# A tuned transformer kernel: the first layer's modulation computed in five parts, and attention queries made two heads ahead with part of the work on GpSimd

## The chip, the cores and the metric

The kernel runs on one core of a Trainium2 chip. The metric is the device time of one launch in microseconds. Three runs of the kernel before gave 2015.85, 2015.19 and 2012.34 us, so the median is 2015.19 us. A difference of 0.2% is 4.0 us.

## The reference, cut to what matters

Two blocks run one after the other on 256 latent and 256 context tokens of width 1024, in float32. The first block has four layers; layer 0 mixes tokens by a Fourier transform, layer 1 by differential attention, layer 2 by latent attention with 16 heads, layer 3 by a Fourier transform again. The second block has one mixer and a mixture of experts. The change touches two places: the modulation vectors of layer 0, and the attention of layer 2.

```python
sh_a, sc_a, g_a, sh_m, sc_m, g_m = split(silu(c) @ mod_w[i] + mod_b[i], 6)   # c: 1024, mod_w[i]: 1024 x 6144
h = rms_norm(x, g_mix) * (1 + sc_a) + sh_a                # shift and scale ahead of the mixer
y = fft2(h, axes=(token, channel within group of 256)).real @ fourier_w + bias     # layer 0
x = x + g_a * y                                           # gate
x = x + g_m * (relu((rms_norm(x, g_mlp) * (1 + sc_m) + sh_m) @ w1) ** 2 @ w2)
# layer 2, for each of 16 heads (96-wide queries and keys, 64-wide values, 256 queries, 512 keys)
p = softmax((q_nope k_nope^T + q_rope k_rope^T) * scale);  o = p @ v
```

The same is computed for the context with silu(c_ctx). The shift of layer 0 is constant over the tokens, so in the transform it reaches only token 0 of the result.

## The kernel before, in words

All activations lie transposed: 128 channels on the partitions, 8 column tiles, 512 tokens (256 latent, 256 context) along the free axis. A float32 product is made from three products of rounded halves (`split_product`, L1847 to L1849: high times high, high times low, low times high). Weights come in 1 MB units of two 128-column panels; ScalarE rounds a panel to its high half (`split_hi`, L1064, 1.05 us), VectorE subtracts for the low half (`split_lo`, L2818, 1.22 us), and TensorE multiplies 24 times per panel. Every engine's program is written out in order, with semaphores; nothing is rescheduled. All loads go through the one queue of SyncE, in the order of its program, each held until its buffer is free.

**Layer 0 before.** The start turns the inputs and normalises the token rows. Then TensorE alternates between `first_rows_product` (L2032; 16 products that fold the tokens) and `mod_unit` (L1890 to L1901): one unit is 1 MB of `mod_w`, 128 input channels by 2048 output columns, as four products of 512 columns in four column groups, put into one PSUM bank. Eight units give shift and scale of the mixer together (group 0). `copy_first_rows` (ScalarE, L1190), `turn_first` (TensorE, L1908) and `first_read` (VectorE, L2982 to L2993) bring them to the partitions. Only then can ScalarE and VectorE scale the folded rows (`G_hi`, L1237, `G_lo`, L3051), with the shift put into two edge columns of each half (`edge`). The transform over channels follows: 8 steps of 12 matmuls, each followed by one unit of group 1 (gate of the mixer and scale of the MLP), while ScalarE copies and rounds (L1250, L1254), VectorE combines cosines and sines (L3071 to L3074) and GpSimd makes the low halves `H_lo` (L1027). Next come the 8 panels of `fourier_w`: panels 0 to 3 whole, panels 4 to 7 once for the latent and once for the context half (`half_outputs`). During them `boundary` on VectorE adds the gated result to x (L2886), sums squares (L2838), splits the next panels and runs `mod_folds` (L2971): a multiply-accumulate of one 128x1024 tile of the transposed `mod_w` with the spread `c`, which makes 128 modulation values for one stream. 32 of these make shift and gate of the MLP in layer 0; 4 stand ahead of `boundary`, 12 in it, 16 in the MLP. The MLP of layer 0 starts with `half_products` on three panels; its first output tile is read at 149.41 us.

SyncE's order before: c and mod_b (3 small loads), x, ctx, units 0 to 2, the other vectors, units 3 and 4, the store of c, dft, units 5 to 15, then the four loads of `fourier_w`, the spread c, 4 units for the folds, and the MLP weights.

**Latent attention before.** A turn for head h does on VectorE: `m_max` of two score tiles (L3493), `query(h+1)` (L3461), a wait for the two exponentials, 1/z (L3502), the scaling of the first half of the probabilities (L3504), `query_lo(h+1)` (L3465), low halves of keys (L3471), of the output of head h-2 (L3514), of the turned probabilities of head h-1 (L3522), in eight places of values (L3477) and after turns 0, 1, 3, 6, 8, 14, 15 a `split_lo` of a panel. ScalarE does the exponentials (L1569), the high halves, and the scaling of the second half of the probabilities (L1577). TensorE makes scores(h) (which wait for `query_lo(h)`), query(h+1), keys, the weighted values of h-2, and turns the probabilities of h-1 (L2396). GpSimd is idle.

Of the kernel before, what the change touches and what calls it, by code (L numbers as in the profile page):

```python
# [6 lines left out]
F32 = mybir.dt.float32  # L7
F32R = mybir.dt.float32r
# [45 lines left out]
def place_vectors():  # L54
    rows = [0] * VEC_TILES
    plan = [("mod_b_lo", 0, 96), ("c", 0, 8), ("c_ctx", 0, 8), ("mod_b_hi", 1, 96),
            ("norm_mix_g", 2, 32), ("norm_mlp_g", 2, 32), ("final_g", 2, 8), ("fourier_b", 2, 16),
# [113 lines left out]
def mla_tiles():  # L171
# [10 lines left out]
    for turn in range(MLA_HEADS - 1):  # L182
        add("q", turn + 1, "mla_q", turn + 2)
# [137 lines left out]

def mla_bank(n):
# [60 lines left out]
FIRST_GROUPS = 2  # L383
FIRST_TILES = MOD_TILES // 3
FIRST_COLS = FIRST_TILES * P
FIRST_PART = FIRST_COLS // 4
FIRST_UNITS = FIRST_GROUPS * KT
FIRST_RING = 3
ROWS_AFTER = {1: range(0, 3), 2: range(3, 6), 3: range(6, 9), 4: range(9, 12), 5: range(12, 14), 6: range(14, 16)}
# [6 lines left out]
LATER_FIRST = {"shift_m": 3 * KT, "gate_m": 5 * KT}  # L396


def place_mods():


    tiles = [(0, t) for part in ("shift_m", "gate_m") for t in range(LATER_FIRST[part], LATER_FIRST[part] + KT)]
# [14 lines left out]
    take("first", [(0, 4)])  # L417
    take("four0", enumerate([2, 2, 2, 2, 1, 1, 1, 1]))
# [25 lines left out]
def build_program(nc, a, out):  # L444
# [8 lines left out]
    with ctx:  # L453
# [51 lines left out]
        first_raw = [sb(f"first_raw{r}", [P, FIRST_COLS], over=work + r * 4 * FIRST_COLS) for r in range(FIRST_RING)]  # L505
        assert FIRST_RING * FIRST_COLS <= MOD_RING * MOD_PAIR * D
        c_all = sb("c_all", [P, 2, D])
        mod_prod = sb("mod_prod", [P, D])
        c_rows = sb("c_rows", [2 * KT, P], over=at["mod_prod"] + 4 * FIRST_PART)
# [12 lines left out]
        edge = norm_buf[3][:, 0:4 * KT].rearrange("p (t e) -> p t e", e=2)  # L522
# [3 lines left out]
        first_rows = sb("first_rows", [P, FIRST_PART], over=at["mod_prod"])  # L526
# [33 lines left out]
        mq_f = sb("mq_f", [P, LAT])  # L560
        mq_hi, mq_lo = sb("mq_hi", [P, LAT], F32R), sb("mq_lo", [P, LAT], F32R)
# [108 lines left out]
        mod_ps = psum[4]  # L670
# [23 lines left out]
        def inner(v, m, st):  # L694

            return v[:, m, st * LAT:(st + 1) * LAT].rearrange("p (e c) -> p e c", e=2)[:, :, 1:]

        def edges(v):

            return v[:, :, :].rearrange("p m (s e c) -> p (m s) e c", s=2, e=2)[:, :, :, 0]  # L700
# [21 lines left out]
        first_w = a["mod_w"][0].rearrange("(k p) (t c) -> k p t c", p=P, t=3 * 2)  # L722
        first_t = [slice(0, 2), slice(2, 5, 2)]
# [26 lines left out]
        def _(sp):  # L750
# [21 lines left out]
            def load_mod(n):  # L772

                if n < MOD_RING:
                    sp.wait_ge(s("first_used"), FIRST_UNITS)
# [11 lines left out]
            def load_mlp(layer, region_free=None):  # L787
# [18 lines left out]
                if layer == 0:  # L806
                    block(0, "w0 w1 w2 m1 w3 m1 w4 w5 m1 w6 m1 w7 m1")
# [25 lines left out]
            rows = {"mod_b_lo": mod_b[0:96], "mod_b_hi": mod_b[96:192],  # L833
# [12 lines left out]
            def load_first(units):  # L846
                for n in units:
                    if n >= FIRST_RING:
                        sp.wait_ge(s("first_used"), n - FIRST_RING + 1)
                    sp.dma_start(first_raw[n % FIRST_RING][:, :].rearrange("p (t c) -> p t c", t=2),  # L850
                                 first_w[n % KT][:, first_t[n // KT], :]).then_inc(s(f"first_in{n % FIRST_RING}"), 16)
# [9 lines left out]
            load_first(range(FIRST_RING, KT - 3))  # L861
            sp.wait_ge(s("c_rows"), 2)
            sp.dma_start(c_store.rearrange("(r c) -> r c", c=P), c_rows[:, :]).then_inc(s("c_all"), 16)
# [3 lines left out]
            load_first(range(KT - 3, KT))  # L867
            four_w = a["fourier_w"][0].rearrange("(k p) (u c) -> u p k c", p=P, c=2 * P)
            load_first(range(KT, FIRST_UNITS))
            for u in range(2):  # L870
                load_unit(PLAN.at["four0"]["unit"] + u, [(whole, four_w[u])])
# [3113 lines left out]
```

## Time and profile before

| | us |
|---|---|
| median of three runs | 2015.19 |
| the profiled execution's own time | 2013.53 |
| its span in the profile | 2011.8 |
| TensorE busy | 1921.9 (96% of the span) |
| VectorE busy | 1531.0 (76%) |
| ScalarE busy | 1018.4 (51%) |
| GpSimd busy | 22.5 (1%) |
| mean granted TensorE clock | 0.984 of full |
| DMA | 346.67 MB, mean 172 GB/s |

The busy shares are over the whole span; a change in one stage has to be read from that stage, so the rows below come from 0 to 150 us (layer 0) and from 1148 to 1258 us (latent attention). Line numbers are those of the kernel before. "PEclk" is the share of full TensorE clock that was granted.

### The profile page before, as it was taken

Reading aid. Unit: us, or ns where it says so; the run is one execution under the profiler, and the core shown is the slowest. Engines: PE = TensorE matmul, PEld = TensorE weight load, DVE = VectorE, ACT = ScalarE, POOL = GpSimd, SP = SyncE. Lnnn points to the kernel's source line nnn. Section 1 sums busy time; section 2 is a strip of 40 time slices with the busy share of each in tenths; the row PEclk is TensorE's granted clock in tenths of the full one; section 3 lists DMA queues with packets and bytes.
Section 4 is the critical chain, followed back from the end, with each engine's and each line's share of the span. In section 5 each row is a group of like instructions: output and inputs, shape, how many; then the busy total and the mean of one; then the engine's idle time right before and its main releaser. Section 6 shows DMA issues by size and latency. Waiting matters only on the chain.

```text
span 2011.8 us, 31051 instructions
## 1 busy us (share of the span) xinstructions
PE 1921.9 (96%) x11602; PEld 1684.5 (84%) x11602; DVE 1531.0 (76%) x2619; ACT 1018.4 (51%) x1721; POOL 22.5 (1%) x40
## 2 busy tenths in 40 slices
PE   6889999999999999999999777999999999999998
PEld 4687888889787888888888667999999999997886
DVE  3689888887667758777777588788887667876796
ACT  5353323245666656232333577655555546655685
POOL 0200000000000000000000100000000000000000
PEclk9999999999999999999999899999999999999999
DMA  7936455541211234557675220677645555426795
GB/s 291 321 119 232 165 209 188 188 168 48 84 64 63 67 112 139 169 186 244 236 244 158 58 73 27 227 268 261 207 135 189 168 169 168 134 67 236 260 354 195
DMA packets 265319, 346.67 MB, mean 172 GB/s; under 512 B 24167, under 2 KB 234962, under 8 KB 263778
## 3 DMA queue, kind: packets, MB, share of 16 engines
q1 hardware_dynamic: 265186, 344.90, 51.2%
q8 instruction: 84, 1.38, 0.3%
q14 instruction: 49, 0.40, 0.1%
HBM read 343.81 MB, written 1.06 MB: 171 GB/s over the span
## 4 chain that ended last, share of the span: by engine, by line
PE 75%; DVE 10%; ACT 6%; issue 5%; SPq 1%; DMA 1%; DVEq 0%; ACTq 0%
PE bank L1847 23%; PE bank L1848 23%; PE bank L1849 23%; PE bank L2663 2%; DVE w_lo L2818 2%; PE bank L2653 1%; ACT p_raw L1401 1%; ACT p_raw L1389 1%; DVE p_all L3297 1%; ACT norm L1157 1%; ACT w_hi L1064 1%; ACT mp_raw L1569 1%; DVE x L2886 1%; DVE neg_max L3306 1%; DVE norm L2844 1%
## 5 line engine op out<-in xcount | busy, mean ns | idle before, releaser
L2818 DVE TENSOR_TENSOR w_lo<-w_raw,w_hi 128x1024 fp32r<-128x1024 f32 x449 | 545.6, 1221 | 51.6 <-ACT w_hi L1064 24.9
L1064 ACT ACTIVATE w_hi<-w_raw 128x1024 fp32r<-128x1024 f32 x350 | 368.0, 1053 | 381.7 <-PE bank L1849 371.2
L1847 PE MATMUL bank<-h_hi,w_hi 128*128 128x512 f32 (+3 forms) x1360 | 466.9, 343 | 14.7 <-DVE w_lo L2818 8.6
L1848 PE MATMUL bank<-h_lo,w_hi 128*128 128x512 f32 (+3 forms) x1360 | 460.3, 338 | 0.0
L1849 PE MATMUL bank<-h_hi,w_lo 128*128 128x512 f32 (+3 forms) x1360 | 459.9, 338 | 0.0
L1847 PE MATMUL bank<-g_hi,w_hi 128*128 128x256 f32 (+1 forms) x1216 | 401.6, 330 | 7.2 <-DVE g_lo L3351 3.6
L1848 PE MATMUL bank<-g_lo,w_hi 128*128 128x256 f32 (+1 forms) x1216 | 399.6, 329 | 0.0
L1849 PE MATMUL bank<-g_hi,w_lo 128*128 128x256 f32 (+1 forms) x1216 | 399.5, 329 | 0.0
L1847 PEld LDWEIGHTS bank<-h_hi,w_hi 128*128 128x128 f32 x1360 | 257.9, 190 | 50.5 <-DVE w_lo L2818 10.8
L1849 PEld LDWEIGHTS bank<-h_hi,w_lo 128*128 128x128 f32 x1360 | 258.1, 190 | 27.7
L1848 PEld LDWEIGHTS bank<-h_lo,w_hi 128*128 128x128 f32 x1360 | 258.2, 190 | 26.4 <-issue 0.3
L1847 PEld LDWEIGHTS bank<-g_hi,w_hi 128*128 128x128 f32 x1216 | 231.8, 191 | 30.2 <-DVE g_lo L3351 4.5
L1849 PEld LDWEIGHTS bank<-g_hi,w_lo 128*128 128x128 f32 x1216 | 231.8, 191 | 20.3
L1848 PEld LDWEIGHTS bank<-g_lo,w_hi 128*128 128x128 f32 x1216 | 231.9, 191 | 19.7
L2971 DVE CUSTOM_DVE_ANT_0 mod_raw<-mod_raw,c_all,vec 128x1024 f32<-128x1024 f32 x160 | 203.0, 1278 | 0.0
L3016 DVE SCALAR_TENSOR_TENSOR x<-bank,mod,x 128x256 f32<-128x256 f32 x192 | 87.4, 479 | 85.1 <-PE bank L1849 79.8
L1304 ACT ACTIVATE norm<-bank 128x512 f32<-128x512 f32 x64 | 38.3, 598 | 189.4 <-PE bank L1849 189.4
L1744 ACT ACTIVATE w_hi<-w_raw 128x1024 fp32r<-128x1024 f32 x99 | 104.1, 1059 | 33.8 <-PE bank L1849 22.5
L3164 DVE TENSOR_TENSOR norm<-norm 128x512 f32<-128x512 f32 (+1 forms) x128 | 71.0, 555 | 54.2 <-ACT norm L1304 49.6
L2971 DVE CUSTOM_DVE_ANT_0 mod_prod<-mod_raw,c_all,vec 128x1024 f32<-128x1024 f32 x80 | 102.2, 1277 | 0.0
L3167 DVE TENSOR_TENSOR g_lo<-norm,g_hi 128x512 fp32r<-128x512 f32 (+1 forms) x128 | 71.5, 559 | 13.6 <-DVE norm L3164 0.5
L1847 PE MATMUL bank<-u_hi,w_hi 128*128 128x258 f32 x256 | 73.5, 287 | 0.0
(535 smaller groups left out, 2832.0 us busy)
## 6 DMA issues: line engine op xcount, KB each, us to landing
w_raw<-in_mlp_w SPq DMA_DIRECT2D x128, 1024.0 KB, 5.4
mod_raw<-in_mod_t SPq DMA_DIRECT2D x80, 1024.0 KB, 7.3
w_raw<-in_w_expert_gate SPq DMA_DIRECT2D x34, 512.0 KB, 4.7
w_raw<-in_w_expert_up SPq DMA_DIRECT2D x34, 512.0 KB, 5.8
w_raw<-in_w_expert_down SPq DMA_DIRECT2D x17, 1024.0 KB, 5.7
first_raw<-in_mod_w SPq DMA_DIRECT2D x16, 1024.0 KB, 5.9
w_raw<-in_diff_w_qkv SPq DMA_DIRECT2D x12, 1024.0 KB, 5.2
w_raw<-in_fourier_w SPq DMA_DIRECT2D x8, 1024.0 KB, 7.9
```

Of the source, the lines that this page charges most:

```text
L1064: act.activation(split_panel(W_hi[n % RING], n), raw_panel(n), ACT.Copy).then_inc(s("w_hi"), 1)
L1304: act.activation(relu[j % 2][:, 0:n_cols], bank[(t0 + j) % BANKS][:, 0:n_cols], ACT.Relu).then_inc(s("relu"), 1)
L1744: act.activation(W_hi[(p0 + n) % RING][:, :], raw_panel(p0 + n), ACT.Copy).then_inc(s("w_hi"), 1)
L1847: pe.matmul(dst, w_hi, r_hi, start=start, stop=False)
L1848: pe.matmul(dst, w_hi, r_lo, start=False, stop=False)
L1849: return pe.matmul(dst, w_lo, r_hi, start=False, stop=stop)
L2663: ins = pe.matmul(slot_out[half][:, :], e[x % 2][:, k, 0:P], v[:, w], start=x % 4 == 0 and k == 0 and q == 0, stop=x % 4 == 3 and k == 1 a ...
L2818: dve.tensor_tensor(split_panel(W_lo[n % RING], n), raw_panel(n), split_panel(W_hi[n % RING], n).bitcast(F32), ALU.subtract).then_inc(s("p ...
L2971: dve.tensor_tensor_reduce(mod_prod[:, :] if again else raw, raw, c_all[:, st, :], 1.0, bias, ALU.mult, ALU.add, mod[layer][:, t, st:st + ...
L3016: ins = dve.scalar_tensor_tensor(X[:, m, c], bank[t % BANKS][:, c], mod[layer][:, gate_at + m, st:st + 1], X[:, m, c], ALU.mult, ALU.add)
L3164: dve.tensor_tensor(squared, relu[j % 2][:, c], relu[j % 2][:, c], ALU.mult).then_inc(s("g_sq"), 1)
L3167: dve.tensor_tensor(G_lo[:, j, c], squared, G_hi[:, j, c].bitcast(F32), ALU.subtract).then_inc(s("g_lo"), 1)
```

## The change

**Layer 0.** The modulation is cut into five parts of 1024 columns in the order scale and shift of the mixer, gate of the mixer, shift and scale of the MLP (`FIRST_PARTS = [KT, 0, 2*KT, 3*KT, 4*KT]`). A unit is still 1 MB but holds 256 input channels by 1024 columns, so a part has 4 units and all have 20 (16 before), and a unit is 8 products of 256 columns in place of 4 of 512. The shift of the MLP is no longer folded on VectorE: 16 folds (4 ahead of `boundary`, 12 in it) are gone; the gate of the MLP stays folded, in the MLP. Units 0 to 6 stand among the row products, unit 7 after step 1 of the transform, units 8 to 19 among the panels. The parts alternate over three banks (psum 4 to 6). The shift goes in by itself: it is multiplied by the DFT matrix (`shift_wave`) and added to the first token's column, which is kept in `first_col` and split apart from the rest; TensorE waits for it (`edge` >= 3) before the first panel. The `edge` steps are gone. ScalarE's split of dft comes after all 16 row copies (after 14 before); four panels are split ahead of `boundary` (three before). The first vector tile takes the two norm vectors too, so 5 small loads stand ahead of x (3 before). SyncE issues the first two `fourier_w` units after unit 7, the other two after unit 10, units 11 to 19 after them, and then the spread c and three fold units behind the first MLP weights.

**Latent attention.** Queries are made two heads ahead with two buffers each. The scaling of the second half of the probabilities goes from ScalarE to GpSimd, and the seven low halves of panels from VectorE to GpSimd.

```diff
-plan = [("mod_b_lo", 0, 96), ("c", 0, 8), ("c_ctx", 0, 8), ...
+plan = [("mod_b_first", 0, 48), ("c", 0, 8), ("c_ctx", 0, 8), ("norm_mix_g", 0, 32), ("norm_mlp_g", 0, 32), ...
+FIRST_PARTS = [KT, 0, 2 * KT, 3 * KT, 4 * KT]
+FIRST_AFTER = {0: [8, 9], 1: [10, 11], 2: [12, 13], 3: [14, 15, 16], 4: [17], 5: [18], 6: [19]}
-ROWS_AFTER = {1: range(0, 3), 2: range(3, 6), 3: range(6, 9), 4: range(9, 12), 5: range(12, 14), 6: range(14, 16)}
+ROWS_AFTER = {1: range(0, 4), 2: range(4, 8), 3: range(8, 12), 4: range(12, 14), 5: range(14, 16)}
-    take("first", [(0, 4)])
-    take("four0", enumerate([2, 2, 2, 2, 1, 1, 1, 1]))
 # SyncE
-            load_first(range(KT - 3, KT))
-            load_first(range(KT, FIRST_UNITS))
+            load_first(range(5, 8))
             for u in range(2):
                 load_unit(PLAN.at["four0"]["unit"] + u, [(whole, four_w[u])])
+            load_first(range(8, 11))
             sp.wait_ge(s("u_lo"), 4 + GROUPS)
             for u in range(2, 4):
                 load_unit(PLAN.at["four0"]["unit"] + u, [(whole, four_w[u])])
+            load_first(range(11, FIRST_EACH * len(FIRST_PARTS)))
+            sp.wait_ge(s("edge"), 3)
 # TensorE
+            def first_unit(n):
+                part, u = n // FIRST_EACH, n % FIRST_EACH
...
+                for i in range(FIRST_STEP):
+                    for j in range(4):
+                        ins = pe.matmul(first_ps[part % 3][32 * j:32 * (j + 1), 0:FIRST_SIDE], silu_c[:, k, :], ...
-                    mod_unit(n, 1)
+                    if n == 1:
+                        first_unit(2 * FIRST_EACH - 1)
+                    if n == 2:
+                        turn_first(1)
+                    if n == 3:
+                        shift_wave()
+                pe.wait_ge(s("edge"), 3)
                 for m in range(4):
                     panel_product(n0 + m, t + m, H_hi, H_lo, ...)
-                    if m == 0:
-                        turn_first(1)
+                    for u in FIRST_AFTER[m]:
+                        first_unit(u)
+                    if m == 1:
+                        turn_first(2)
 # VectorE, end of the transform
-                for n in range(1, AHEAD):
+                dve.wait_ge(s("wave"), 1)
+                dve.wait_ge(s("four_sum"), KT)
+                for half in range(2):
+                    dve.scalar_tensor_tensor(col, wave, DFT_N ** 0.5, col, ALU.mult, ALU.add).then_inc(s("edge"), 1)
+                split_lo_at(p0 + 1)
+                dve.wait_ge(s("first_col"), 1)
+                dve.tensor_tensor(first_tokens(H_lo), first_col, first_tokens(H_hi), ALU.subtract).then_inc(s("edge"), 1)
+                for n in range(2, RING):
                     split_lo_at(p0 + n)
 # GpSimd, latent attention
+            for turn in range(MLA_HEADS):
+                pool.wait_ge(s("z_inv"), BEFORE_MLA["z_inv"] + turn + 1)
+                pool.tensor_scalar(mp_raw[turn % 2][1][:, :], mp_raw[turn % 2][1][:, :], m_zinv[:, turn % 2, 1:2], None,
+                                   ALU.mult).then_inc(s("mla_norm1"), 1)
+                for n in MLA_SPLITS.get(turn, []):
+                    pool.wait_ge(s("w_hi"), p0 + n + 1)
+                    pool.tensor_tensor(split_panel(W_lo[r], p0 + n), raw_panel(p0 + n), ..., ALU.subtract)
 # VectorE, ScalarE, TensorE, latent attention
-                    if turn + 1 < MLA_HEADS:
-                        query(turn + 1)
+                    if turn + 2 < MLA_HEADS:
+                        query(turn + 2)
```

## Rows read from the trace of the kernel before

**Rows 1.** The page: busy us, share of the span and instructions of each engine.
```profile
PE 1921.9 (96%) x11602; PEld 1684.5 (84%) x11602; DVE 1531.0 (76%) x2619; ACT 1018.4 (51%) x1721; POOL 22.5 (1%) x40
```
**Rows 2.** Stretch, its us, busy us of PE, PEld, DVE, ACT, POOL, PEclk, DMA share, GB/s.
```profile
45.00:51.00 6.00, 5.95 (x25) 4.09 (x26) 2.54 (x9) 1.54 (x5) 0.00 (x0) 0.50 0.06 10
...
69.50:73.65 4.15, 0.00 (x1) 0.01 (x1) 1.28 (x2) 1.61 (x3) 0.00 (x0) 0.74 1.09 349
...
90.00:122.00 32.00, 25.32 (x155) 22.64 (x155) 30.70 (x54) 8.81 (x13) 0.00 (x0) 0.95 0.67 230
```
**Rows 3.** Waits from 0 to 220 us: who waited for whom, total, times, longest.
```profile
PE bank L1847 <- DVE w_lo L2818: 8.6, 5, 4.2
...
ACT w_hi L1064 <- DMA w_raw<-in_fourier_w: 6.3, 1, 6.3
```
**Rows 4.** SyncE's queue in order of time: start, us, the transfer issued.
```profile
5.82 0.47 SPq L843 DMA_DIRECT2D vec_rows<-in_norm_mix_g  x1
6.33 0.42 SPq L843 DMA_DIRECT2D vec_rows<-in_norm_mlp_g  x1
...
61.41 9.64 SPq L761 DMA_DIRECT2D w_raw<-in_fourier_w  x4
```
**Rows 5.** Folds in 90 to 122 us, one row of two forms.
```profile
L2971 DVE CUSTOM_DVE_ANT_0 mod_raw<-mod_raw,c_all,vec 128x1024 f32<-128x1024 f32 x7 | 8.9, 1277 | 0.0
```
**Rows 6.** The chain of waits in order of time, one of eight modulation units in the transform.
```profile
57.30 1.00 PE bank L1899 x8
```
**Rows 7.** ScalarE's and VectorE's instructions in order of time, end of the row products.
```profile
36.42 1.05 ACT L1221 ACTIVATE dft_hi<-dft 128x1024 fp32r<-128x1024 f32 x1
...
37.50 1.23 DVE L3272 TENSOR_TENSOR dft_lo<-dft,dft_hi 128x1024 fp32r<-128x1024 f32 x1 [12.67 <-ACT dft_hi L1221]
...
42.66 1.70 ACT L1237 ACTIVATE g_hi<-four_raw,scale_mix 128x254 fp32r<-128x254 f32 x4 [1.66 <-issue]
```
**Rows 8.** The same view, VectorE's last four scaled low halves in the transform.
```profile
59.97 2.70 DVE L3051 SCALAR_TENSOR_TENSOR g_lo<-four_raw,scale_mix,g_hi 128x254 fp32r<-128x254 f32 x4 [1.10 <-ACT g_hi L1237]
```
**Rows 9.** Instructions in order of time: GpSimd and VectorE at one time.
```profile
52.33 1.28 POOL L1027 TENSOR_TENSOR h_lo<-norm,h_hi 128x512 fp32r<-128x512 f32 x1 [50.33 <-ACT h_hi L1254]
...
52.72 0.91 DVE L3073 TENSOR_TENSOR norm<-norm 128x2 f32<-128x2 f32 x1
53.55 0.15 DVE L3074 TENSOR_TENSOR norm<-norm 128x2 f32<-128x2 f32 x1
```
**Rows 10.** VectorE in latent attention, in order of time: first, three middle, last turn.
```profile
1152.14 0.69 DVE L3493 TENSOR_REDUCE m_max<-bank 128x1 f32<-128x512 f32 x1 [1.07 <-PE bank L1849]
...
1220.30 1.28 DVE L3493 TENSOR_REDUCE m_max<-bank 128x1 f32<-128x512 f32 x2
...
1225.85 1.28 DVE L3493 TENSOR_REDUCE m_max<-bank 128x1 f32<-128x512 f32 x2
...
1228.25 0.49 DVE L3504 TENSOR_SCALAR mp_raw<-mp_raw,m_zinv 128x512 f32<-128x512 f32 x1
1228.65 0.42 DVE L3465 TENSOR_TENSOR mq_lo<-mq_f,mq_hi 128x256 fp32r<-128x256 f32 x1
...
1231.95 1.28 DVE L3493 TENSOR_REDUCE m_max<-bank 128x1 f32<-128x512 f32 x2
...
1250.07 1.28 DVE L3493 TENSOR_REDUCE m_max<-bank 128x1 f32<-128x512 f32 x2
```
**Rows 11.** Groups by line in latent attention: busy, mean ns, idle before and releaser.
```profile
L1847 PE MATMUL bank<-mk_hi,mq_hi 128*128 128x512 f32 x31 | 14.3, 461 | 13.7 <-DVE mq_lo L3465 13.7
...
L1577 ACT ACTIVATE mp_raw<-mp_raw,m_zinv 128x512 f32<-128x512 f32 x16 | 11.5, 720 | 0.4 <-DVE m_zinv L3502 0.2
...
L2818 DVE TENSOR_TENSOR w_lo<-w_raw,w_hi 128x1024 fp32r<-128x1024 f32 x7 | 8.6, 1225 | 0.6
...
L3477 DVE TENSOR_TENSOR h_lo<-bank,h_hi 128x512 fp32r<-128x512 f32 x8 | 5.3, 681 | 0.3 <-ACT h_hi L1551 0.3
```
**Rows 12.** ScalarE in order of time: the first output tile of the MLP of layer 0.
```profile
149.41 0.60 ACT L1304 ACTIVATE norm<-bank 128x512 f32<-128x512 f32 x1 [1.18 <-PE bank L1849]
```

More of the change, by code:

```diff
@@ L181, in mla_tiles @@
     add("k", 0, "mla_k_lo", 2)
-    for turn in range(MLA_HEADS - 1):
-        add("q", turn + 1, "mla_q", turn + 2)
+    add("q", 1, "mla_q", 2)
+    for turn in range(MLA_HEADS - 2):
+        add("q", turn + 2, "mla_q", turn + 3)
         if turn % 2 == 0 and turn // 2 + 1 < MLA_HEADS // 2:
@@ L395 @@
 MOD_STEPS = {}
-LATER_FIRST = {"shift_m": 3 * KT, "gate_m": 5 * KT}
 def place_mods():
-    tiles = [(0, t) for part in ("shift_m", "gate_m") for t in range(LATER_FIRST[part], LATER_FIRST[part] + KT)]
+    tiles = [(0, t) for t in range(5 * KT, MOD_TILES)]
     tiles += [(layer, t) for layer in range(1, DEPTH) for t in range(MOD_TILES)]
@@ L521, in build_program @@
         row_sum, row_inv = o_sum[:, 0:4], o_inv[:, 0:4]
-        edge = norm_buf[3][:, 0:4 * KT].rearrange("p (t e) -> p t e", e=2)
+        first_rows = [sb(f"first_rows{r}", [P, FIRST_SIDE], over=at["mod_prod"] + 2048 + r * 4 * FIRST_SIDE) for r in range(2)]
+        first_col = sb("first_col", [P, KT, 2])
         lam_in = sb("lam_in", [1, 4, HALF])
@@ L1169, in boundary @@
                         square(name, TOK, m - 1, x0 + m)
+                    if m == 0 and name == "mlp0":
+                        copy_first_rows(2)
                 split_hi(n0 + 4 + AHEAD)
@@ L1595, in mla_attention @@
                         values(i)
-                    for n in splits.get(turn, []):
+                    for n in MLA_SPLITS.get(turn, []):
                         if n == 4:
@@ L1888, in first_products @@
                         norm_sum(*norm)
-            def mod_unit(u, g):
-                if u == 0 and g:
-                    pe.wait_ge(s("mod_read"), g)
-                n = KT * g + u
-                pe.wait_ge(s(f"first_in{n % FIRST_RING}"), 16 * (n // FIRST_RING + 1))
-                for j in range(4):
-                    ins = pe.matmul(mod_ps[32 * j:32 * (j + 1), 0:FIRST_PART], silu_c[:, u, :],
-                                    first_raw[n % FIRST_RING][:, j * FIRST_PART:(j + 1) * FIRST_PART],
-                                    start=(u == 0), stop=(u == KT - 1))
-                ins.then_inc(s("first_used"), 1)
@@ new lines, in turn_first, with shift_wave @@
+            def turn_first(part):
+                pe.wait_ge(s("first_rows"), part + 1)
+                for j in range(FIRST_SIDE // P):
+                    ins = pe.transpose(first_ps[part % 3][:, j * P:(j + 1) * P], first_rows[part % 2][:, j * P:(j + 1) * P],
+                                       ident[:, :])
+                ins.then_inc(s("first_turned"), 1)
+            def shift_wave():
+                pe.wait_ge(s("mod_sum"), 2)
+                for half in range(2):
+                    for k in range(2):
+                        ins = pe.matmul(wave_ps[:, half * KT:(half + 1) * KT], dft[:, 2 * k, half * P:(half + 1) * P],
+                                        mod[0][:, k:KT:2, :], start=(k == 0), stop=(k == 1))
+                ins.then_inc(s("wave"), 1)
@@ L1961, in half_outputs @@
                         ins.then_inc(s("half_done" if st == 0 else "tile_done"), 1)
+                        if name == "mlp0" and st == 0:
+                            for u in FIRST_AFTER.get(m, []):
+                                first_unit(u)
+                            if m == 5:
+                                turn_first(3)
+                            if m == KT - 1:
+                                turn_first(4)
             def half_products(n0, t0, name):
@@ L2895, in boundary @@
                         add_square(name, TOK, m - 1)
-                    mod_folds(*folds(m))
+                    if name == "mix1":
+                        mod_folds(("mlp", 0, BLOCKS - 1), KT + m)
                 split_lo_at(n0 + 4 + AHEAD)
@@ L2903, in boundary @@
                     add_square(name, LAT, m - 1, 0)
-                    mod_folds(*folds(m))
                 add_square(name, LAT, KT - 1, 0)
+                if name == "mlp0":
+                    first_read(3)
+                    first_read(4)
                 if name == "mix1":
@@ L3524, in mla_attention @@
                         values(i)
-                    for n in splits.get(turn, []):
-                        split_lo_at(p0 + n)
             norm_rest("mix2", TOK)
```

255 lines of the change are left out of this document (129 added, 126 removed).

## The prediction

> **What bounds the kernel now.** I read the page first. TensorE is busy for 96% of the span, so a change can win only where TensorE idles or runs at its lower clock, and whatever it adds to TensorE in a full stretch costs its whole length [rows 1]. Then the busy time by stretch in layer 0 [rows 2]. Three holes stand there. From 69.5 to 73.65 us TensorE does nothing. From 90 to 122 us it is busy for 25.3 of 32 us, an idle 6.7, while VectorE is busy for 30.7: that stretch is bound by VectorE. And the granted clock is 0.50 from 45 to 51 us (the 1.2 GHz level of 2.4, after four almost idle microseconds), and 0.95 on average in 90 to 122, which is 32 x 0.05 = 1.6 us of lost work. The waits name the causes: TensorE waits for low halves of panels, 4.2 us at once, and behind it ScalarE waits 6.3 us for `fourier_w` [rows 3]. SyncE issues that load only at 61.41, behind all sixteen modulation units [rows 4]. In 90 to 122 us the folds take 7 x 1.28 us in one of their two forms, 14 in all [rows 5]: 18 of VectorE's 31 us.
>
> In latent attention VectorE leads: turns without a panel split take 5.55 us (from 1220.30 to 1225.85) or 6.10 us (to 1231.95), the 15 turns from 1152.14 to 1250.07 take 97.9 us, and TensorE waits 13.7 us for the low half of the query [rows 10, 11].
>
> **Ahead of the transform.** Two more small loads, 0.5 us apart, stand ahead of x [rows 4]; the first row product waits for ctx behind x, so everything shifts by +0.95. In the stage of row products one unit fewer stands: a unit takes 1.0 us [rows 6], with the change of operands about 1.2, so -1.2. The turn of part 0 comes behind the twelfth product, and TensorE waits there for a row copy and the copy of the sums: +0.9 of waiting and 0.35 of transposes where the old turn was after everything. The last row copy ends some 0.7 us later than before, at 39.85. Now ScalarE's split of dft (1.05) comes after it, then VectorE's (1.15 of 1.23 until the next can start), then the reading of part 0 (0.4): the first scaled row at 42.45 in place of 42.66 [rows 7]. The early scale is thus hidden by nothing: the dft split takes its place as the last wait. With the edge steps gone the transform starts at about 44.75, after 45.05: -0.3 so far. TensorE still idles nearly 4 us ahead of it, so I leave the slow clock of 45 to 51 as it is.
>
> **The transform.** Seven of eight units leave it, 8.4 us of TensorE. But the steps hang on ScalarE (per two steps: four scalings 1.7, copies 0.7, roundings 1.2, 3.6 us) and on VectorE, whose four low halves take 2.70 us beside GpSimd [rows 8], and TensorE only catches up with them. The last scaled rows come at about 61.05, 1.7 us ahead of 62.7. Then, in order: sums of steps 4 and 5 (1.6), first panel high and low (2.2), sums of 6 and 7 (1.6), the wave added (0.4), first tokens rounded (0.25), panel 1 high (1.05) and low (1.2), first tokens' low half (0.2): 8.5 us of instructions and, with semaphores and GpSimd in the way once, 9.4 to 11. The first panel starts between 70.5 and 72.1; I take 71.3 against 73.65. So of the 4.2 us hole, which the earlier `fourier_w` load closes, most comes back as the wait for `edge` >= 3, behind which all panels queue. Up to here: -2.35. The slow clock after the hole stays, since the hole stays.
>
> **The panels.** The 16 folds leave (4 ahead of `boundary`, 12 in it), and with them the idle 6.7 us and the 1.6 us of slow clock [rows 2]: -8.3. But twelve units now stand here, on an engine with no idle time left to hide them: 12 x 1.2 = +14.4. A unit has twice as many matmuls of half the width; the ends are 1.0 us, the row of before, and 2.0 us, if each matmul keeps its time [rows 6]; 1.2 lies nearest the row, since the columns streamed are the same. Three turns replace one, with a wait of 0.5 for the copy of part 2: +1.0. The panels: +7.1, with ends of +4.7 and +16.7. DMA hides: each unit is issued when the third before it is used, 7 us or more ahead of its own use, except 17 to 19, where it is about 6; if that cover goes it is 1 or 2 us. In the MLP behind it nothing moves: its folds and the first weights stand as far ahead of their use as before. Layer 0 in sum: -2.35 + 7.1 = +4.75.
>
> **Latent attention.** The seven splits leave VectorE: 7 x 1.15 = 8.0 us [rows 11]. Queries two heads ahead end the wait of 13.7 us on TensorE; that saves VectorE only what it waits itself, the 0.55 by which every second turn is longer [rows 10]. The new 15 turns, at 5.55, plus eight value splits of 0.6 [rows 11], less 1.45 for the shorter turns 0, 1 and 14, are 86.6 us: -11.3. ScalarE loses 16 scalings of 0.72, 0.62 apart [rows 11]; at the end, where TensorE waits for the last low halves, this gives 0.8: -12.1. Against it stands the new neighbour. In the transform a VectorE addition of two columns with both inputs in SBUF, 0.15 us right behind it, took 0.91 us, from 52.72 to 53.63, while a GpSimd subtraction ran from 52.33 to 53.61 [rows 9]: it waited for GpSimd's end. The new GpSimd scaling becomes free to start at 1/z, as VectorE's own scaling does (1228.25), and right behind that stands the low half of the query (1228.65, both inputs in SBUF) [rows 10]. So VectorE waits for GpSimd's whole scaling, in every turn. Nothing in the trace is that scaling. The ends are 0, if GpSimd is late and slips in behind the query's low half, and 1.28 us, the two-input row of the same shape [rows 9]; I take 0.75, above half of that row, as it reads one input in place of two. 15 x 0.75 = +11.2. The GpSimd splits, 2.6 us each, fall on instructions of VectorE that read PSUM: nothing. Attention: -0.9, with ends of -12.1 and +7.1.
>
> The Trainium skill, SBUF — State Buffer, section Who interferes with whom, says the two share a port pair as an exclusive lock, held for the instruction, against VectorE instructions with two SBUF inputs or in a two-port mode; the 0.91 us agrees, and it speaks against this change. The Trainium skill, GPSIMD Engine Reference, section 3.1, gives a two-input loop 2.6 cycles per element and the shortest one-input bodies 1.03, at 1.2 GHz: 0.44 us for 512 elements, an estimate without dispatch. By it attention would come to -12.1 + 6.6 = -5.5 and the kernel to no gain or loss; no row here shows it.
>
> **The sum.** +4.75 - 0.9 = +3.9 us. The profiled execution took 2013.53 (span 2011.8 and 1.7 around it), so 2017.4; the median of the runs is 1.7 above that execution, so the prediction is 2019.1.
>
> **The rivals.**
> - Slower clearly: GpSimd's scaling takes the full 1.28 and VectorE pays it in 15 turns. For it: rows 9. Against: one input. It decides above 0.81 us (12.1 / 15), where attention turns into a loss. +7.1 + 4.75 = +11.9: 2027.
> - Faster clearly: GpSimd slips in behind the query's low half, so the lock costs nothing. For it: a start only 0.4 us late does it. Against: GpSimd started 0.1 us after its releaser in the transform. -12.1 + 4.75 = -7.4: 2007.8.
> - Layer 0 does better: the transform runs with TensorE ahead and the first panel starts at 68.5, and a unit costs 1.0. For it: the row of 1.0. Against: the list of instructions behind the last scaled rows. -5.1 + 4.7 = -0.4, attention -0.9 to -5.5: 2011 to 2014.
> - The stall only moves: units 14 to 19 arrive late behind `fourier_w` and each other, 1 us each: +6 more, 2025. For it: DMA at 1.09 of its share in the hole [rows 2]; against: three buffers ahead.
>
> **How the numbers follow.** Forecast 0.40 (own range 2015 to 2023), slower rival 0.18, faster rival 0.15, better layer 0 0.17, late units 0.10. What a measurement of this kernel can tell from no change is 0.2%, 4 us: 2011.2 to 2019.2. The forecast lies at that edge and gives half its chance to each side, so slower is 0.20 + 0.18 + 0.10 = 0.48, less 0.06 for what I may have missed in favour: 0.42; faster is 0.15, 0.05 of the third rival and those 0.06: 0.26; the same 0.32. The range of 2007 to 2027 runs from the faster to the slower rival and leaves out less than 2 in 10.
>
> **What would show it.** TensorE's first panel near 71 us, led by the low half of the first tokens; VectorE no longer full in the panels, TensorE without idle time there, and `half_products` some 5 us later (first tile of the MLP read near 154 us, before at 149.4 [rows 12]). In attention turns of 6.3 us, all alike, with the query's low half over 1 us long. The prediction is wrong if the panels start before 69 us, if the first MLP tile is read before 150, or if turns are 5.6 us (faster) or 6.8 (slower).

## The result, and the profile after

The changed kernel takes 2001.07 us (median of 4 runs, 2000.89 to 2001.83), the kernel before 2013.76 (median of 4): a ratio of 0.9932, 95% interval 0.992 to 0.9945. That is 12.7 us less. I had forecast 2019.1, in a range from 2007 to 2027: wrong in sign and outside the range. (My forecast stood on three runs of the kernel before; the fourth lowers their median from 2015.19 to 2013.76.)

The page of the changed kernel, its engine line (busy us, share of the span, instructions):
```profile
PE 1921.4 (96%) x11804; PEld 1689.5 (85%) x11804; DVE 1501.7 (75%) x2573; ACT 1006.8 (50%) x1705; POOL 72.1 (4%) x63
```
TensorE is busy for as long as before [rows 1], in a span of 1999.3 us in place of 2011.8, so what left is idle time. GpSimd went from 22.5 to 72.1 us.

The same stretches as in [rows 2], and latent attention (stretch, its us, busy us of PE, PEld, DVE, ACT, POOL, PEclk, DMA share, GB/s):
```profile
69.50:73.65 4.15, 2.77 (x7) 2.19 (x8) 3.60 (x4) 1.33 (x2) 0.15 (x1) 0.50 0.00 0
90.00:122.00 32.00, 30.56 (x272) 23.75 (x271) 16.53 (x38) 7.37 (x13) 0.00 (x0) 1.00 0.89 325
1152.00:1257.00 105.00, 93.10 (x618) 82.65 (x618) 81.63 (x169) 69.57 (x159) 49.90 (x23) 0.98 0.15 49
```
In the panels VectorE has gone from 30.70 to 16.53 busy us, and TensorE's 6.7 idle us are 1.4. In latent attention TensorE is busy for 93.1 of 105 us (84.5 before).

To see where the time went I set equal instructions of the two traces side by side and took the difference of their starts. Behind layer 0 the changed kernel is 3.3 us late (first MLP tile, below, against [rows 12]). Ahead of latent attention it is 5.3 us late. Behind it, from the MLP of layer 2 on, it is 10.4 us early, so attention gave 15.7 us. At the end it is 12.5 early. So 2.0 us were lost and 2.1 won in places where nothing was changed.

The 2.0 us between layers 0 and 2 lie in two such places. Here are those stretches, of the changed kernel and then of the one before:
```profile
516.00:560.00 44.00, 40.88 (x221) 32.74 (x222) 30.03 (x72) 29.42 (x70) 0.00 (x0) 0.96 0.15 49
630.00:680.00 50.00, 49.25 (x271) 40.83 (x270) 35.44 (x76) 33.16 (x77) 0.00 (x0) 0.93 0.19 64
```
```profile
516.00:560.00 44.00, 39.54 (x230) 31.53 (x226) 30.84 (x74) 28.64 (x69) 0.00 (x0) 1.00 0.16 50
630.00:680.00 50.00, 48.33 (x284) 39.19 (x285) 36.32 (x77) 35.39 (x84) 0.00 (x0) 1.00 0.20 64
```
The granted clock was 1.00 before and 0.96 and 0.93 after, over unchanged instructions that start 3 to 5 us later. It does not go with the change: `layer0` and `dft_spread` (below), which have layer 0's part too, show 1.00 in both stretches, while `attn_scale_act` and `attn_low_later`, whose layer 0 is that of the kernel before, show 0.96 in the first. (The 0.93 of the second stretch stands in two of the five kernels with layer 0's part, and in none of the others.) The 2.1 us won back are mostly the same thing the other way round: from 1640 to 1665 us the kernel before has a granted clock of 0.93, the changed one has 1.00 over the same instructions and gains 1.5 us there. What makes the clock fall in one execution and not in another is not shown. A single trace tells parts apart only down to some 2 us unless one looks at this column.

Layer 0 of the changed kernel in order of time (start, us, engine, line, tiles, idle time before and its releaser): a unit pair in the panels, the late unit, and the first MLP tile:
```profile
70.88 0.80 PE L1866 MATMUL bank<-h_hi,w_hi 128*128 128x512 f32 x1 [7.13 <-DVE h_lo L3120]
...
86.75 1.93 PE L1920 MATMUL bank<-first_raw,silu_c 128*32 128x256 f32 x32
...
109.87 1.07 PE L1920 MATMUL bank<-first_raw,silu_c 128*32 128x256 f32 x16 [1.44 <-DMA first_raw<-in_mod_w]
```
```profile
152.74 0.60 ACT L1328 ACTIVATE norm<-bank 128x512 f32<-128x512 f32 x1 [1.19 <-PE bank L1868]
```

And one turn of latent attention, VectorE and then GpSimd, for [rows 10]. Turns in which VectorE makes no low half of values take 5.27 and 5.51 us (plain turns, below). From VectorE's first row maximum (`m_max`, one pair in each turn) to the sixteenth it is 82.9 us, 97.9 before:
```profile
1222.65 0.17 DVE L3548 RECIPROCAL m_zinv<-m_z 128x2 f32<-128x2 f32 x1 [0.58 <-ACT mp_raw L1592]
1222.85 0.49 DVE L3550 TENSOR_SCALAR mp_raw<-mp_raw,m_zinv 128x512 f32<-128x512 f32 x1
1223.25 0.42 DVE L3509 TENSOR_TENSOR mq_lo<-mq_f,mq_hi 128x256 fp32r<-128x256 f32 x1
1223.70 0.69 DVE L3516 TENSOR_TENSOR mk_lo<-bank,mk_hi 64x512 fp32r<-64x512 f32 x1
...
1225.97 1.28 DVE L3539 TENSOR_REDUCE m_max<-bank 128x1 f32<-128x512 f32 x2
```
```profile
1222.91 2.11 POOL L1048 TENSOR_SCALAR mp_raw<-mp_raw,m_zinv 128x512 f32<-128x512 f32 x1 [3.14 <-DVE m_zinv L3548]
...
1239.21 1.86 POOL L1048 TENSOR_SCALAR mp_raw<-mp_raw,m_zinv 128x512 f32<-128x512 f32 x1 [3.41 <-DVE m_zinv L3548]
```
GpSimd's scaling runs from 1222.91 to 1225.02, longer than I had allowed at its worst (1.28), and VectorE works beside it as if it were not there: the low half of the query takes 0.42 us as before. GpSimd is the slower one for it: 2.11 us where that low half stands beside it, 1.86 and 1.85 in the last two turns, which have none.

### The profile page after: what moved, and what is told of

It is laid out like the page before. It is cut to its first block, busy times and chain, and to the rows that moved or that the text cites. A ratio compares the mean times of both kernels' runs of the same rounds, so it can differ in the third digit from the quotient of the medians.

```text
span 1999.3 us, 31406 instructions
## 1 busy us (share of the span) xinstructions
PE 1921.4 (96%) x11804; PEld 1689.5 (85%) x11804; DVE 1501.7 (75%) x2573; ACT 1006.8 (50%) x1705; POOL 72.1 (4%) x63
## 4 chain that ended last, share of the span: by engine, by line
PE 79%; DVE 10%; ACT 5%; issue 4%; DMA 1%; POOL 1%; SPq 0%; DVEq 0%; ACTq 0%
PE bank L1866 24%; PE bank L1867 23%; PE bank L1868 23%; PE bank L2712 2%; PE bank L2702 1%; DVE w_lo L2867 1%; ACT p_raw L1424 1%; PE bank L1920 1%; ACT p_raw L1412 1%; ACT norm L1173 1%; DVE p_all L3341 1%; ACT mp_raw L1592 1%; DVE mpt_lo L3568 1%; DVE norm L2893 1%; ACT w_hi L1080 1%
## 5 line engine op out<-in xcount | busy, mean ns | idle before, releaser
L2867 DVE TENSOR_TENSOR w_lo<-w_raw,w_hi 128x1024 fp32r<-128x1024 f32 x442 | 538.0, 1223 | 44.0 <-ACT w_hi L1763 21.9
L3019 DVE CUSTOM_DVE_ANT_0 mod_raw<-mod_raw,c_all,vec 128x1024 f32<-128x1024 f32 x152 | 192.9, 1279 | 0.0
L3019 DVE CUSTOM_DVE_ANT_0 mod_prod<-mod_raw,c_all,vec 128x1024 f32<-128x1024 f32 x72 | 92.0, 1278 | 0.0
```

The source lines that it names most:

```text
L2867: dve.tensor_tensor(split_panel(W_lo[n % RING], n), raw_panel(n), split_panel(W_hi[n % RING], n).bitcast(F32), ALU.subtract).then_inc(s("p ...
L3019: dve.tensor_tensor_reduce(mod_prod[:, :] if again else raw, raw, c_all[:, st, :], 1.0, bias, ALU.mult, ALU.add, mod[layer][:, t, st:st + ...
```

## The experiments

Times are medians; ratios are against the kernel before, run beside them, with their 95% interval. The runs were made in four batches, in which the median of the kernel before was 2013.66 to 2014.67 us. So a difference of two medians from different batches is good to about 1 us.

**The two parts apart.** `layer0` and `attn` are the kernel before with one part of the diff each.

> The kernel before with the layer 0 part of the change alone, latent attention as before. If the 3.3 us that stand behind layer 0 in the changed kernel's trace are this part's price: before plus 3.3, 2017. The forecast on record said plus 4.75. A further 2 us appear between 510 and 650 us of that trace, where nothing was changed and the granted clock was 0.98 against 1.00: if they belonged to the change, this kernel would be 5.3 us slower, 2019; I expect them to be absent or as large in the kernel before of another execution.

Measured: 2017.08 us, ratio 1.0019 (1.0009 to 1.0029). Its trace is 3.3 to 3.4 us late from the first MLP on, up to latent attention.

> The kernel before with the latent attention part of the change alone: queries two heads ahead, GpSimd scaling the second half of the weights and splitting the seven panels. Layer 0 is as before. From the trace of the changed kernel (first ScalarE tile of layer 3's attention 5.3 us later than before, the first MLP tile behind it 10.4 us earlier) I expect 15.7 us less than before, 1998. My forecast on record gave this part 0.9 us, its faster rival 12.1 us (2001.7). First and sixteenth maxima of VectorE 83 us apart, low half of a query 0.42 us long.

Measured: 1997.09 us, ratio 0.9916 (0.9903 to 0.9929). The first and sixteenth maxima are 83.2 us apart. The parts add up: layer 0 costs 3 to 4 us, attention gives 16 to 17. All the gain is in attention. `attn` alone is 4.0 us under the changed kernel, though the intervals of the two ratios overlap.

**Does GpSimd hold VectorE?**
`attn_two_inputs` is `attn` with the scaling on GpSimd written in another form, with 1/z as a second tensor:
```
-                pool.tensor_scalar(mp_raw[turn % 2][1][:, :], mp_raw[turn % 2][1][:, :], m_zinv[:, turn % 2, 1:2], None,
-                                   ALU.mult).then_inc(s("mla_norm1"), 1)
+                pool.tensor_tensor(mp_raw[turn % 2][1][:, :], mp_raw[turn % 2][1][:, :],
+                                   m_zinv[:, turn % 2, 1:2].to_broadcast([P, TOK]), ALU.mult).then_inc(s("mla_norm1"), 1)
```


> As attn, but GpSimd scales by a tensor_tensor with 1/z broadcast, so that it reads two inputs from SBUF, and not by a tensor_scalar. Theory (the form of GpSimd's instruction decides: two tensors from SBUF hold VectorE, one does not): the low half of a query, 0.42 us in attn, lasts until GpSimd's end, 0.9 us or more, and a turn is 0.5 us or more longer: 7 to 8 us slower than attn, about 2006. Rival (GpSimd gives way to VectorE whatever its form): low half 0.42 us, turns of 5.3 to 5.5 us as in attn, the same time; it would be up to nothing but GpSimd's own length.

Measured: 2012.08 us, ratio 0.9989 (0.998 to 0.9999), 15 us over `attn`. VectorE and GpSimd in one turn:
```profile
1202.74 0.17 DVE L3517 RECIPROCAL m_zinv<-m_z 128x2 f32<-128x2 f32 x1 [0.59 <-ACT mp_raw L1585]
1202.94 1.37 DVE L3519 TENSOR_SCALAR mp_raw<-mp_raw,m_zinv 128x512 f32<-128x512 f32 x1
1204.23 0.41 DVE L3478 TENSOR_TENSOR mq_lo<-mq_f,mq_hi 128x256 fp32r<-128x256 f32 x1
```
```profile
1202.99 1.04 POOL L1048 TENSOR_TENSOR mp_raw<-mp_raw,m_zinv 128x512 f32<-128x512 f32 x1 [1.12 <-DVE m_zinv L3517]
```
GpSimd starts 0.05 us behind VectorE, as in `attn` (0.06), yet now VectorE's own scaling takes 1.37 us in place of 0.49 and ends 0.28 us behind GpSimd. That is so in fifteen of the sixteen turns, and fifteen times 0.88 is 13.2; the turns are 96.4 us together in place of 83.2. In the first turn GpSimd starts 0.12 us behind VectorE's scaling, and there it is the other way round: VectorE keeps its 0.49 us, and GpSimd takes 1.27. I had named the wrong victim, the query's low half, and so the size was too small (7 to 8), but the theory stands: the form of GpSimd's instruction decides. GpSimd's two-input form is also the faster one for GpSimd, 1.04 against 1.86 to 2.11 us.

`attn_two_after` is `attn_two_inputs` with GpSimd's start moved:
```
-                pool.wait_ge(s("z_inv"), BEFORE_MLA["z_inv"] + turn + 1)
+                pool.wait_ge(s("mla_norm0"), turn + 1)
+                pool.wait_ge(s("qk_lo"), BEFORE_MLA["qk_lo"] + min(turn + 3, MLA_HEADS))
```


> As attn_two_inputs, but GpSimd starts its scaling only behind VectorE's scaling and the query's low half, the two instructions of VectorE in the turn whose tensors all lie in SBUF; what VectorE does meanwhile reads a bank. Theory (GpSimd's two-input instruction holds only VectorE's instructions that work from SBUF alone): VectorE's scaling is 0.49 us again, its other instructions keep their lengths, GpSimd's scaling takes 1.04 us and ends no later than the 2.1 us one of attn: turns of 5.3 to 5.5 us and the time of attn, 1997 (1996 to 1998). Rival (the hold is against anything VectorE does): mk_lo or the halves behind it are up to 1 us longer, turns of 6.1 us or more, about 2012.

Measured: 1997.62 us, ratio 0.9918 (0.9905 to 0.993), turns of 5.26 and 5.51:
```profile
1211.88 0.48 DVE L3520 TENSOR_SCALAR mp_raw<-mp_raw,m_zinv 128x512 f32<-128x512 f32 x1
1212.28 0.42 DVE L3479 TENSOR_TENSOR mq_lo<-mq_f,mq_hi 128x256 fp32r<-128x256 f32 x1
1212.61 0.68 DVE L3486 TENSOR_TENSOR mk_lo<-bank,mk_hi 64x512 fp32r<-64x512 f32 x1
1213.21 0.41 DVE L3530 TENSOR_TENSOR g_lo<-bank,g_hi 64x256 fp32r<-64x256 f32 x1
```
```profile
1212.84 1.04 POOL L1049 TENSOR_TENSOR mp_raw<-mp_raw,m_zinv 128x512 f32<-128x512 f32 x1 [4.48 <-DVE mq_lo L3479]
```
The same instruction of GpSimd, beside instructions of VectorE that read a bank, holds nobody. The price is one of placement: 15 us at one point of the turn, nothing that can be told 0.9 us later in it.

**What the scaling was worth on ScalarE.** `attn_scale_act` takes GpSimd's scaling out of `attn` again and gives it back to ScalarE, as below; `scale_alone` puts GpSimd's scaling alone into the kernel before:
```
                     if turn // 2 + 1 < MLA_HEADS // 2:
                         keys(turn // 2 + 1, turn % 2)
+                    if on:
+                        act.wait_ge(s("z_inv"), BEFORE_MLA["z_inv"] + turn + 1)
+                        act.activation(mp_raw[turn % 2][1][:, :], mp_raw[turn % 2][1][:, :], ACT.Identity,
+                                       scale=m_zinv[:, turn % 2, 1:2]).then_inc(s("mla_norm1"), 1)
```


> As attn, but the second half of the weights is scaled on ScalarE, as in the kernel before. ScalarE gets 16 x 0.72 us back, ahead of the panels' and outputs' high halves. If VectorE's own instructions make the turn (theory), ScalarE's 0.72 comes out of its idle 0.9 to 1.9 us of each turn and costs at most where the low halves of the turned weights wait: 0 to 4 us over attn, 1998 to 2002. Rival (moving the scaling is what brought most): 8 us or more over attn, turns of 5.8 us and longer.

Measured: 2006.26 us, ratio 0.9965 (0.9952 to 0.9978), 9.2 over `attn`: the rival that I had not believed. Turns of 5.55 and 6.10 us are back, as in the kernel before, though the queries are two ahead. VectorE and ScalarE in one:
```profile
1201.19 0.69 DVE L3486 TENSOR_TENSOR mk_lo<-bank,mk_hi 64x512 fp32r<-64x512 f32 x1
1202.22 0.43 DVE L3530 TENSOR_TENSOR g_lo<-bank,g_hi 64x256 fp32r<-64x256 f32 x1 [0.33 <-ACT g_hi L1596]
1202.84 1.29 DVE L3538 TENSOR_TENSOR mpt_lo<-bank,mpt_hi 128x512 fp32r<-128x512 f32 x2 [0.20 <-ACT mpt_hi L1605]
```
```profile
1201.06 0.72 ACT L1590 ACTIVATE mp_raw<-mp_raw,m_zinv 128x512 f32<-128x512 f32 x1
1201.81 0.38 ACT L1596 ACTIVATE g_hi<-bank 64x256 fp32r<-64x256 f32 x1
1202.21 1.09 ACT L1605 ACTIVATE mpt_hi<-bank 128x512 fp32r<-128x512 f32 x2
```
ScalarE's scaling stands in its queue ahead of the high halves of the output and of the turned weights, and VectorE's low halves wait for those: the waits of 0.33 and 0.20 us. From the start of `mk_lo` to the next maximum a turn takes 2.41 or 2.86 us here; in `attn` it takes 2.12 or 2.27. That is all of the 0.3 and 0.6 us by which the turns differ. ScalarE's idle time, 1.5 us ahead of the next turn's exponentials, comes too late to help. The trace of the kernel before had the same two waits, and I had not read them:
```profile
1230.12 0.43 DVE L3514 TENSOR_TENSOR g_lo<-bank,g_hi 64x256 fp32r<-64x256 f32 x1 [0.33 <-ACT g_hi L1583]
1230.74 1.29 DVE L3522 TENSOR_TENSOR mpt_lo<-bank,mpt_hi 128x512 fp32r<-128x512 f32 x2 [0.19 <-ACT mpt_hi L1592]
```

> The kernel before with one edit: the second half of the weights is scaled on GpSimd (one-input form) and not on ScalarE. Theory (ScalarE's scaling stands ahead of the high halves that VectorE waits for, and GpSimd's does not hold VectorE): plain turns of 5.3 and 5.5 us in place of 5.55 and 6.1, VectorE's first to sixteenth maxima some 90 us apart in place of 97.9, 6 to 9 us under before: about 2006. My forecast on record credited this edit with 0.8 us at the end and charged it 11.2: by that it would be 10 us slower than before, 2024.

Measured: 2006.67 us, ratio 0.9959 (0.9946 to 0.9972), 7.5 under the kernel before; plain turns of 5.26 and 5.51, 92.3 us from the first maximum to the sixteenth (some 90 expected). So it came about as expected.

**The other two edits of attention**, each taken back in `attn`.

> As attn, but VectorE splits the seven panels, as in the kernel before. Both theories give VectorE 7 x 1.15 = 8.0 us back in attention; where VectorE sets the turn that is 8 us over attn, 2005. If a part hides in the 0.58 us for which VectorE waits in each turn, it is 4 to 8.

Measured: 2005.47 us, ratio 0.995 (0.9937 to 0.9964), 8.4 over `attn`, or 7.4 if each is taken against the kernel before of its own batch.

> As attn, but the queries are made one head ahead, as in the kernel before (GpSimd still scales and splits). Theory: VectorE's own list and ScalarE's high halves make the turn, and the wait of TensorE for the low half of the query was never VectorE's: up to 0.55 us a turn at most, 0 to 4 us over attn, 1997 to 2001. Rival (the earlier queries brought much of the 16.6 us): 8 us or more over attn.

Measured: 1998.55 us, ratio 0.9918 (0.9904 to 0.9931), 1.5 over `attn`, or 0.5 against the kernels before: not told apart. Its turns are the same 5.26 and 5.51. Apart, then: splits 7.4 to 8.4, scaling 7.5 to 9.2, queries 1.5 at most.

**What ends last in a turn now.** In `attn` VectorE still waits 0.58 us for the second exponential. `attn_low_later` moves the query's low half in front of that wait:
```
                     if turn + 2 < MLA_HEADS:
                         query(turn + 2)
+                    if 1 <= turn < MLA_HEADS - 1:
+                        query_lo(turn + 1)
...
-                    if turn + 2 < MLA_HEADS:
-                        query_lo(turn + 2)
```


> As attn, but the low half of each query is taken one turn later, between the float query and the reciprocal, where VectorE waits 0.58 us in every turn for the second exponential. If VectorE's list makes the turn: 0.42 less in each of 14 turns, 5.8 us under attn, 1991. If TensorE (busy 4.9 of each 5.4 us turn) or the loop of maximum, exponential and reciprocal is next: 1 to 4 us under attn.

Measured: 1997.44 us, ratio 0.991 (0.9895 to 0.9925): no gain that can be told. Plain turns fall only to 5.12 and 5.39, and the fifteen together to 82.9 from 83.2:
```profile
1218.50 0.41 DVE L3478 TENSOR_TENSOR mq_lo<-mq_f,mq_hi 128x256 fp32r<-128x256 f32 x1
1219.16 0.17 DVE L3519 RECIPROCAL m_zinv<-m_z 128x2 f32<-128x2 f32 x1 [0.26 <-ACT mp_raw L1585]
1219.36 0.49 DVE L3521 TENSOR_SCALAR mp_raw<-mp_raw,m_zinv 128x512 f32<-128x512 f32 x1
1220.09 0.69 DVE L3485 TENSOR_TENSOR mk_lo<-bank,mk_hi 64x512 fp32r<-64x512 f32 x1 [0.24 <-ACT mk_hi L1563]
```
The wait for the exponential shrinks and one for ScalarE's next high half appears. VectorE (busy for 60.5 of 65 us from 1170 to 1235), TensorE (60.9) and ScalarE's order are now close together. This run also shows who pays for whom beside GpSimd's tensor_scalar: with the query's low half gone from beside it, GpSimd's scaling takes 1.86 us in place of 2.11 in all plain turns:
```profile
1219.42 1.86 POOL L1048 TENSOR_SCALAR mp_raw<-mp_raw,m_zinv 128x512 f32<-128x512 f32 x1 [3.24 <-DVE m_zinv L3519]
```

**Layer 0.** My own step said that the dft split was the last wait ahead of the transform. `dft_spread` is the changed kernel with two repairs, `vec_later` adds a third:
```
                     if n == KT + 3:
                         copy_first_rows(0)
-                act.wait_ge(s("dft_in"), 32)
-                act.activation(dft_hi[:, :, :].rearrange("p k (a c) -> p (k a) c", a=2), dft[:, :, :],
-                               ACT.Copy).then_inc(s("dft_hi"), 1)
+                        act.wait_ge(s("dft_in"), 32)
+                        act.activation(dft_hi[:, :, :].rearrange("p k (a c) -> p (k a) c", a=2), dft[:, :, :],
+                                       ACT.Copy).then_inc(s("dft_hi"), 1)
...
-FIRST_AFTER = {..., 3: [14, 15, 16], 4: [17], 5: [18], 6: [19]}
+FIRST_AFTER = {..., 3: [14, 15], 4: [16, 17], 5: [18], 6: [19]}
```


> The changed kernel (both parts), with two repairs in layer 0. ScalarE splits dft at once behind the first copy of the sums, at 34 us where it idles for 2.4 us, and not behind the last row copy at 40.2; and unit 16 moves from behind the fourth panel to behind the fifth, so that unit 17 does not wait 1.4 us for its transfer. My own step said that the dft split is the last wait ahead of the transform: if so the transform starts at about 43 in place of 45.3 us, the first panel at 68.7 in place of 70.9, and with unit 17 in time the kernel is 3.5 us faster than the changed one, 1997.5. Rival (TensorE, or the slow clock moving along, takes it back): 0 to 1 us faster.

Measured: 1997.71 us, ratio 0.9911 (0.9897 to 0.9925), 3.4 under the changed kernel, with intervals that overlap. The trace gives it 2.0 at the first MLP: 1.1 from an earlier transform (44.22), and 0.9 behind it, which fits unit 17, whose wait falls from 1.44 to 0.44. The expectation of 43 was wrong, and ScalarE's rows name why: the vector copy, which waits for TensorE, stood next in its queue.
```profile
34.29 1.06 ACT L1244 ACTIVATE dft_hi<-dft 128x1024 fp32r<-128x1024 f32 x1
...
40.18 0.38 ACT L1239 ACTIVATE four_raw<-bank 128x256 f32<-128x256 f32 x1 [0.33 <-PE bank L1868]
41.50 0.40 ACT L1249 ACTIVATE vec<-bank 128x96 f32<-128x96 f32 x2 [0.94 <-PE bank L2209]
41.79 3.29 ACT L1260 ACTIVATE g_hi<-four_raw,scale_mix 128x256 fp32r<-128x256 f32 x8
```

`vec_later` lets ScalarE copy the vectors behind the first four scaled rows.

> As dft_spread, and ScalarE copies the vectors (0.4 us, which waited 0.9 us for TensorE) behind the first four scaled rows instead of ahead of them. In dft_spread the scales were there at 36.9 us, yet the first scaled row stood at 41.8, behind that copy, and the transform started 1.1 us earlier, not 2.3. If the copy was what held it: first scaled row at 40.5, transform at 43.0, 1.1 us under dft_spread, 1996.5. Rival (VectorE's low halves or TensorE's own list are next): no change.

Measured: 1995.12 us, ratio 0.9906 (0.9892 to 0.992): the lowest median of all kernels here, 6 us under the changed one, whose interval its own just touches; it is not told apart from `attn`. The transform starts at 43.16, as expected, 1.1 ahead of `dft_spread`. But the first panel starts at 67.38, which is 2.4 ahead of `dft_spread` (69.81; 70.88 in the changed kernel). The clock differs too. Here are the changed kernel and `vec_later` from 45 to 51 us, for [rows 2]:
```profile
45.00:51.00 6.00, 5.67 (x41) 4.98 (x42) 3.79 (x13) 2.50 (x7) 0.86 (x1) 0.72 1.04 395
```
```profile
45.00:51.00 6.00, 5.82 (x53) 4.70 (x51) 4.06 (x12) 3.90 (x10) 2.56 (x2) 1.00 1.05 398
```
The granted clock of that stretch was 0.50 in the kernel before, 0.72 in the changed one, 0.74 in `dft_spread` and 1.00 in `vec_later`. TensorE had idled for 3.35, 3.79, 2.44 and 1.24 us ahead of the transform. (`both_repaired` repeats the 1.24 and the 1.00; `layer0` idles for 3.79 like the changed kernel and has 0.51.) How much of the other 1.3 us the clock gave is not tested. The first MLP tile is read at 148.8, 0.6 ahead of the kernel before: in this trace layer 0 no longer costs anything.

> vec_later with GpSimd's two-input scaling behind VectorE's own, as in attn_two_after. If both theories hold: the time of vec_later or up to 1 us under it, 1996, which is under the changed kernel (2001.1) and the kernel before. If the two-input form still holds VectorE: 10 us or more over vec_later.

Measured: 1997.31 us, ratio 0.9914 (0.99 to 0.9929). The two-input form behind VectorE's own does no harm here either, but no good: not told apart from `vec_later`, `dft_spread` or `attn`.

## Why the prediction was wrong

The forecast lay 18.0 us above the measured median: 14.8 by attention, 1.4 by layer 0, 1.7 by the median of three runs that I had added to the profiled execution, and the rest is rounding and the clock.

**Attention, -0.9 forecast, -15.7 measured.** Three steps failed.

"So VectorE waits for GpSimd's whole scaling, in every turn": 15 x 0.75 = +11.2, measured nothing. The observation behind it [rows 9] was right, and the changed kernel repeats it in the transform: an addition of two columns takes 0.78 us, until 51.44, beside GpSimd's subtraction, which ends at 51.42, and 0.15 elsewhere. But I took a price from a two-input instruction of GpSimd and halved it for a one-input one, as if the hold were proportional to work. `attn_two_inputs` and `attn` differ in that form alone: 0.88 us a turn or none. My rival in which "GpSimd slips in behind the query's low half" had the right sum for that term and the wrong mechanism, so its closeness there is luck: GpSimd started 0.06 us behind VectorE's scaling, and it was GpSimd that took longer. What in the two forms makes the difference is not shown. The Trainium skill, SBUF — State Buffer, section Who interferes with whom, gives the shared pair to whichever of the two issues first, for the whole instruction. Beside the tensor_tensor the trace shows such a hold: of VectorE in fifteen turns, though by the trace VectorE had started 0.05 us ahead (starts on GpSimd are rough), and of GpSimd in the first turn. Beside the tensor_scalar, which had run for 0.34 us when the query's low half came, VectorE is not held and GpSimd is only 0.25 us longer, so there the measurement decides against a full hold. The Trainium skill, GPSIMD Engine Reference, section 3.1, by which I had estimated 0.44 us for a one-input form without its dispatch, does not agree either: 1.86 us.

"ScalarE loses 16 scalings of 0.72, 0.62 apart", which at the end "gives 0.8": alone it gave 7.5. I had taken ScalarE for an engine with time to spare (in the trace before it is busy for 76.5 of 105 us), and looked only at the tail. The question was what stands behind the scaling in its queue and who waits for that: the high halves for which VectorE waited 0.33 and 0.19 us.

The queries ahead: "that saves VectorE only what it waits itself, the 0.55 by which every second turn is longer". The sum gave this 3.3 us (11.3 less the splits' 8.0). With queries two ahead and the scaling on ScalarE the turns still alternate between 5.55 and 6.10: the 0.55 came from ScalarE's queue, not from the query. The big wait of 13.7 us [rows 11] belonged to TensorE, which was not last in the turn: taking it away is worth 1.5 us at most.

Right were the splits (8.0 forecast, 7.4 to 8.4 measured) and that GpSimd's own splits, 2.4 us each, cost VectorE nothing where they fall on instructions that read a bank.

**Layer 0, +4.75 forecast, +3.3 measured.** The mechanism held in nearly every step. Transform at 44.75 forecast, 45.33 measured. Last scaled rows 61.05, measured 60.5. First panel 71.3, measured 70.88, led by the low half of the first tokens, as said. The hole stays, as said: 7.1 idle us stand ahead of the first panel. In the panels VectorE is no longer full, and the idle time but for unit 17's and the low clock are gone. The term that was mis-sized is the unit: 1.2 us, measured 0.96 (1.93 for two); 12 x 0.24 is 2.9 us too much, of which the wait of unit 17 (1.44) takes half back. That leaves 5.6 for the panels, and measured from the first panel to the first MLP tile it is 6.1; where the other 0.5 lies is open. I had written "if that cover goes it is 1 or 2 us" for units 17 to 19 and left it out of the sum. The granted clock of 45 to 51 us, which I had left as it was, came to 0.72 here and to 0.51 in `layer0`, with the same 3.79 idle us ahead of it; so that part goes with the execution. First MLP tile about 154, measured 152.7, not under the 150 that would have refuted it.

**The chances.** With the measured attention, my layer 0 would have given 2004.3 (2013.53 + 1.7 + 4.75 - 15.7). The faster side had 0.26, and 2001 lay outside the range, since both ends of attention left out what ScalarE's queue could give; that term had no bounds of its own. Turns of 5.27 and 5.51 us lay beyond even the 5.6 that I had named as the sign of the faster rival. One of the rivals was also added up wrongly: with -0.4 in layer 0 and -0.9 to -5.5 in attention, "layer 0 does better" comes to 2009.3 to 2013.9, not 2011 to 2014, so more of its chance belonged to the faster side.

## What to carry to other kernels

For every instruction taken off an engine, ask what stands behind it in that queue and who waits for that; an engine's idle time elsewhere in the turn doesn't hide it. Where work goes to GpSimd beside VectorE, price the neighbour by the same form of instruction, and if it holds VectorE up, move it beside instructions that read a bank before giving it up. A long wait on one engine is worth only what the engine that ends the turn gets of it.

## What the runs showed of the hardware

- GpSimd's scaling of 128x512 from SBUF took 1.86 to 2.11 us as tensor_scalar and 1.04 as tensor_tensor with a broadcast input: the form with one tensor was the slower. It took 1.86 where the query's low half did not stand beside it.
- Beside the tensor_scalar VectorE kept its lengths (0.49, 0.42 us). Beside the tensor_tensor its one-input scaling took 1.37, until 0.28 us behind GpSimd's end, in fifteen turns of sixteen; in the first turn it kept its 0.49, and GpSimd took 1.27. Beside the same tensor_tensor, instructions that read a bank kept theirs (0.68, 0.41).
- The granted clock fell to 0.93 and 0.96 in stretches with unchanged instructions and stayed at 1.00 in another execution, worth 2 us in all, in either direction.
- From 45 to 51 us the granted clock was 1.00 in the two kernels where TensorE had idled for 1.24 us ahead of the transform, and 0.74 behind 2.44 idle us, 0.72 and 0.51 behind 3.79, 0.50 behind 3.35.
